# mLSTM and MLP boundaries of a two-block transformer kernel: result banks claimed later, scaled copies ahead of the next weight half, the first weight unit taken tile by tile over two columns

## What is computed

```python
for l in range(DEPTH):
    ada = cond @ ada_w[l] + ada_b[l]
    sh1, sc1, g1, sh2, sc2, g2 = jnp.split(ada, 6, axis=-1)
    h = modulate(rmsnorm(x, norm_g[l, 0]), sh1, sc1)       # x * (1 + scale) + shift
    if l < N_A:
        y = mlstm_mixer(h, ...)      # q, k, v, gates = h @ w_in; recurrence; (hh * sigmoid(og)) @ w_out
    else:
        y = mla_mixer(h, ...)
    x = x + g1[:, None, :] * rmsnorm(y, norm_g[l, 1])
    h = modulate(rmsnorm(x, norm_g[l, 2]), sh2, sc2)
    y = jnp.square(jax.nn.relu(h @ mlp_w1[l])) @ mlp_w2[l]  # 1024 -> 4096 -> 1024
    x = x + g2[:, None, :] * rmsnorm(y, norm_g[l, 3])
```

## Time and profile before

| | us |
|---|---|
| median of 3 runs | 1192.52 |
| lowest, highest | 1192.41, 1194.96 |
| the profiled execution, span from its first to its last instruction | 1188.7 |
| PE busy (matmuls) | 1099.4 |
| DVE busy | 741.1 |
| ACT busy | 500.7 |
| PE, mean granted clock | 0.977 of full |

### The profile page before, as it was taken

The page is one execution under the profiler, slowest core; times in us unless marked ns, Lnnn a source line. Parts: engine busy times, 40 slices in busy tenths (PEclk is TensorE's granted clock), DMA queues, the critical chain, the costliest instruction groups (busy, mean ns, idle before and its releaser), DMA issues.

```text
span 1188.7 us, 19624 instructions
## 1 busy us (share of the span) xinstructions
PE 1099.4 (92%) x8492; PEld 899.8 (76%) x8492; DVE 741.1 (62%) x1145; ACT 500.7 (42%) x774; POOL 33.3 (3%) x30
## 2 busy tenths in 40 slices
PE   3999978899899997999999899999899898999997
PEld 2885468897668776877767699899757676998995
DVE  4662676864758958575567758767446566555544
ACT  3311312123354466445354545535243644554442
POOL 0000003310000010000000000000000000000000
PEclk9999989999999999899999999999999989999999
DMA  9373400520346550254433486776643534565520
GB/s 387 130 300 135 150 1 3 204 85 4 141 155 271 211 214 1 81 191 176 190 142 142 151 330 235 291 289 262 261 164 142 213 142 142 212 224 202 203 82 36
DMA packets 15078, 204.88 MB, mean 172 GB/s; under 512 B 1800, under 2 KB 1800, under 8 KB 2832
## 3 DMA queue, kind: packets, MB, share of 16 engines
q1 hardware_dynamic: 14256, 201.33, 44.9%
q10 hardware_dynamic: 736, 2.30, 0.5%
HBM read 202.57 MB, written 1.05 MB: 171 GB/s over the span
## 4 chain that ended last, share of the span: by engine, by line
PE 75%; DVE 15%; ACT 4%; DMA 3%; issue 2%; ACTq 0%; DVEq 0%
PE bank L432 15%; PE bank L434 15%; PE bank L433 15%; PE bank L391 6%; PE bank L677 5%; PE bank L479 5%; DMA ring<-in_stream 3%; DVE slot_parts L1721 2%; PE bank L536 2%; PE bank L506 1%; PE bank L492 1%; ACT arena L1266 1%; DVE arena L1835 1%; PE bank L659 1%; DVE small L1695 1%
## 5 line engine op out<-in xcount | busy, mean ns | idle before, releaser
L432 PE MATMUL bank<-page_parts 128*128 128x512 f32 (+1 forms) x1152 | 393.3, 341 | 10.9 <-DVE page_parts L1754 3.2
L1721 DVE TENSOR_TENSOR slot_parts<-ring,page_parts 128x2048 fp32r<-128x2048 f32 x104 | 237.0, 2289 | 124.3 <-ACT page_parts L1173 124.0
L1173 ACT ACTIVATE page_parts<-ring 128x2048 fp32r<-128x2048 f32 x104 | 197.5, 1909 | 142.2 <-PE bank L434 88.0
L432 PEld LDWEIGHTS bank<-page_parts 128*128 128x128 f32 x1152 | 221.3, 192 | 36.2 <-issue 9.1
L433 PE MATMUL bank<-slot_parts,page_parts 128*128 128x512 f32 x576 | 225.0, 391 | 0.0
L434 PE MATMUL bank<-page_parts 128*128 128x512 f32 x576 | 225.0, 391 | 0.0
L1232 ACT ACTIVATE arena<-bank 128x512 f32<-128x512 f32 (+1 forms) x142 | 78.9, 572 | 224.8 <-PE bank L479 66.6
L433 PE MATMUL bank<-page_parts 128*128 128x256 f32 x576 | 164.8, 286 | 0.0
L434 PE MATMUL bank<-page_parts,slot_parts 128*128 128x256 f32 x576 | 164.7, 286 | 0.0
L434 PEld LDWEIGHTS bank<-page_parts 128*128 128x128 f32 x576 | 108.5, 188 | 23.1
L433 PEld LDWEIGHTS bank<-slot_parts,page_parts 128*128 128x128 f32 x576 | 108.6, 189 | 21.3
(11 more groups left out here) (272 smaller groups left out, 1162.4 us busy)
## 6 DMA issues: line engine op xcount, KB each, us to landing
ring<-in_stream SPq DMA_DIRECT2D x95, 2048.0 KB, 8.2
arena<-in_x SPq DMA_DIRECT2D x2, 512.0 KB, 6.2
gn<-in_gn ACTq DMA_DIRECT2D x2, 512.0 KB, 8.5
out<-arena SPq DMA_DIRECT2D x2, 512.0 KB, 2.6
cc<-in_consts ACTq DMA_DIRECT2D x1, 898.0 KB, 6.2
pc<-in_params ACTq DMA_DIRECT2D x1, 287.5 KB, 7.2
gn<-in_head_sel ACTq DMA_DIRECT2D x1, 32.0 KB
pos_i<-in_positions ACTq DMA_DIRECT2D x1, 1.0 KB, 7.1
```

Of the source, the lines that this page charges most:

```text
L432: mm(out, a[0], b[0], start=start, stop=False)
L1173: act(unit_parts(n)[0], unit_values(n)[1], ACT.Copy).then_inc(ac.step("w_hi"), 1)
L1721: tt(unit_parts(n)[1], lo, hi, ALU.subtract).then_inc(dv.step("w_lo"), 1)
```

## The change

Five edits:

1. A new helper `both_halves` issues the first unit of a stage's first product: for each tile k it waits for the tile if needed, does the three products for the first column half and then for the second, and goes on to the next tile. It is used for the first unit of q2 and of `("up", l, 0)`, 48 matmuls each; the number of matmuls is the same. Only the very first matmul of the bank opens it (`start`).
2. In an MLP the claims of banks 0 to 3 are moved from ahead of the first matrix to the first `down`.
3. In an MLP ACT does its eight scaled copies first and the rounding copy of the unit two ahead after them; the copy of the turned columns (L1240) stays behind both.
4. At the mLSTM input the explicit rounding copy `split(ahead(("q2", 0)))` is taken out; the loop that follows the scaled copies does it anyway, now behind the turned columns.
5. On DVE the second unit of `wo_c` is cut right behind `h2T`, ahead of the modulation and the diagonal.

```diff
+            def both_halves(b, W, src, wait):
+
+                for k in range(KT):
+                    pe.wait_ge(sem(wait[0]), wait[1] + k // 2 + 1)
+                    for half in range(2):
+                        out, w, a = b[:, half * T:(half + 1) * T], [w[:, k, half * P:(half + 1) * P] for w in W], [a[:, k, :] for a in src]
+                        mm(out, w[0], a[0], start=k == half == 0, stop=False, skip_group_check=True)
+                        mm(out, w[0], a[1], start=False, stop=False, skip_group_check=True)
+                        ins = mm(out, w[1], a[0], start=False, stop=k == KT - 1, skip_group_check=True)
+                return ins
+
             def split_T(name, src, pages, wait=None, between=None):
...
-                    for half in range(2):
+                    if wait and i == 0:
+                        ins = both_halves(b, W, src, wait)
+                    for half in range(0 if not wait or i else 2, 2):
                         for k in range(KT):
-                            if wait and i == half == 0:
-                                pe.wait_ge(sem(wait[0]), wait[1] + k // 2 + 1)
...
                 rotation["banks"] = [4, 5, 6, 7]
-                for tb in range(TB):
-                    for half in range(2):
-                        claim(("mlp", l, tb, half), 2 * tb + half)
...
                 def down(n):
                     split_panel(("w2", l, n), (3, 4, 14))
+                    if n == 0:
+                        for tb in range(TB):
+                            for half in range(2):
+                                claim(("mlp", l, tb, half), 2 * tb + half)
...
             def mlp(l):
+                mod_scaled(f"hT_m{l}", (1, 4)[l], hT2)
                 split(unit_of["up", l, 0, 0] + AHEAD)
-                mod_scaled(f"hT_m{l}", (1, 4)[l], hT2)
                 ada_turned()
...
             x_squares("wo_b")
-            split(ahead(("q2", 0)))
             ada_direct()
...
             split_h("h2T", H2_PAGES)
+            split(unit_of["wo_c", 0] + 1)
             modulation(6, 12, (1,))
             gate_diagonal(1)
             split(unit_of["wo_c", 1] + 1)
```

## The result

The changed kernel runs in 1177.39 us (median of 4 runs, 1176.87 to 1179.65), beside 1193.74 for the kernel before on the same chip; the ratio is 0.9866, with a 95% interval of 0.9853 to 0.9879. The direction was right and the size was not: 1180.7 was forecast, with a range down to 1178.7. Over all executions measured in the study, before has a mean of 1192.5 (84 runs, 1186.2 to 1198.1), the changed kernel 1177.9 (10 runs, 1175.4 to 1180.9): 14.6 us, uncertain by 1.2, where 11.8 were forecast. One execution of edit 3 alone took 2211.36 us, with PE busy for 2169.9 us under a recorded granted clock of 1.00; it is left out of every figure here and was not explained. The profiled execution of the changed kernel has a span of 1175.1 beside 1188.7, 13.6 less.

What follows compares the result with a forecast made beforehand. The prediction took PE's own time to bound the kernel, with idle at the boundaries removable: 8.2 us of waits plus 3.6 of clock, 11.8 off 1192.5, gave 1180.7 us, with a range of 1178.7 to 1184.4.

Steps and rivals of the forecast that it cites:

- What bounds the kernel: Whole kernel: PE makes up 75% of the chain, DVE 15%; a boundary is worth what PE idles there.
- mLSTM input: Ahead of q2: scaled copies start at 511.0, q2 2.7 us earlier, and 1.2 of half clock goes.
- the tile-by-tile order: First units of q2 and both MLPs: costs nothing, keeps 1.05 us of tile stalls per boundary from coming back.
- Output product: mLSTM layer's output product: PE's wait of 1.36 us for a weight unit goes wholly, taken as 1.4.
- The MLPs: Both MLP inputs: PE starts 2.0 and 2.1 us earlier, and 1.2 of half clock goes at each.
- gives its start back: Rival, first MLP: PE waits at the third panel and loses at most 2.0 + 1.2; 1183.9 us, chance 0.10.
- Clock at the boundaries: mLSTM input and both MLP starts: half-clock stretches go, 1.2 us each, 3.6 in all.
- The rivals in which the half clock stays: At both MLPs, 1183.1 us, or at the mLSTM input too, 1184.3; chance together 0.22.
- Gaps and clock further on fall elsewhere: Rival, loop over the heads: the half-clock stretch behind 576 goes, 1.7 us more, 1179.0; chance 0.12.
- the base: Starting time of the sum: profiled span 1188.7 plus 3.8 us taken as unchanged, so gains come off 1192.5.

Runs made afterwards that it cites:

- claims_only: The kernel before with only the claims of banks 0 to 3 moved to the first `down` in each MLP: ratio 0.9959, 4.9 us faster.
- copies_first_look: The kernel before with only the MLPs' scaled copies put ahead of the rounding copy, executed again for its profile: idle 3.66 and 3.78; first execution's ratio 1.0024.
- before_filled: The kernel before with unread extra matmuls in its large gaps, including those at the mLSTM input and both MLP inputs: 1184.40 us, ratio 0.9943.
- the filled one: The changed kernel with unread extra matmuls in its remaining large gaps: 1172.75 us, ratio 0.9839 to the kernel before.

## Why the prediction was wrong

**What bounds the kernel: right.** Each place that it named as PE's idle gave its time, and nothing outside them became late. The other engines' busy times are the same within 0.1 us.

**mLSTM input: right.** Forecast 2.7 of wait and 1.2 of clock, 3.9; measured 2.56 at the start (516.01 to 513.45) and 1.34 in the 48 matmuls behind it (7.16 to 5.82), 3.90. That the sum fits to the digit is luck: the wait was 0.1 too high and the clock 0.1 too low. The scaled copies began at 511.09, forecast 511.0; the low part of the next unit is ready at 519.0, forecast 519.1. That the tile-by-tile order costs nothing and keeps about 1.0 a boundary from coming back (1.05 in the prediction, 0.98 measured) holds: nothing alone, 2.9 of stalls with the rest.

**Output product: right in its wait, 0.3 short.** The idle went wholly, and the stage gained 1.65 where the row shows 1.36. Two parts make the difference. The idle of a row is counted from the end of the matmul before it, which lasts 0.39, while the next one usually starts after 0.23: 0.16 more. And the first matmul behind the gap has its follower after 0.33 (636.43 to 636.76) where 0.23 is usual: 0.10 more. 1.36 + 0.16 + 0.10 = 1.62. I had counted the idle alone.

**The MLPs: right.** 3.36 and 3.40 where 3.2 and 3.3 stood. In the first the wait gave 1.87 for 2.0 and the clock 1.49 for 1.2, in the second 2.06 for 2.1 and 1.40 for 1.2. PE began the first 0.16 behind DVE's first cut; shifted by the 7.20 gained before it, that is 666.61, forecast 666.5. The claims were the wait, as claims_only shows, and edit 3 needs edit 2, as copies_first_look shows; edit 2 alone leaves 0.65 and 0.44 of idle. The rival "gives its start back" did not come true: from the mark of 681.75 to a matmul at 850.13 before takes 168.38, the changed kernel from 671.19 to 839.64 takes 168.45. The rest of the 0.36 of the table's fifth row lies behind the first MLP and is within what one profile differs from another: from the 97th matmul of the first MLP to the transposes of the second's input, two profiles of before take 310.6 and 312.1, four of the changed kernel 310.8 to 311.1.

**Clock at the boundaries: right in kind, small in size.** The prediction took 13 slow matmuls, 1.2 us, at each, from one trace. Over the profiles that have those gaps the counts are 12 to 27 at q2, some 16 to 24 at the first MLP, 13 to 16 at the second. Against the changed kernel's 5.82 the first 48 matmuls take on average 1.56, 1.65 and 1.47 us longer, 4.7 in all where 3.6 was forecast; in the first profile of before it is 4.2. The rivals in which the half clock stays are out: it is full at all three in all four profiles of the changed kernel. The Trainium skill, "TensorE: Matmul & The Clock Gate", Part 4, would have kept all three, since transposes don't count as PE being busy; the trace doesn't agree with what I drew from it: behind 1.97 us of transposes and 1.05 of turned columns the clock is 1.00 at 513 to 515.

**What failed is the clock term of the sum, above all the stretch in the loop over the heads, which was put at nothing.** "Gaps and clock further on fall elsewhere", with the stretch behind 576 worth 1.7, was given 0.12 and kept out of the forecast. It was worth 1.65 in the profile of the changed kernel, and with 9 in 10 against 1 in 4 it is worth some 1.1 on average. The three boundaries, written as 3.6, gave 4.2 in the first profile and 4.7 on average. I had read one trace of before as if its half-clock stretches were fixed parts of it. They are draws: behind the same 1.72 at 342 and the same 1.17 at 576 the half clock is there in one execution and not in the next, and the kernel's own runs reach from 1186.2 to 1198.1 for the same program. The range made the same mistake. Its lower end, 1178.7, lay only 0.3 below the case that gives up the heads' stretch, while 0.5 of clock at the boundaries was missing too and the median is itself uncertain by about one.

The account: 12.0 from the two traces without the heads, which holds 4.2 of clock, 0.5 more for the mean of 4.7, and 1.1 for the heads is 13.6 of the 14.6 measured. Most of the last 1.0 may be chance in a part where no edit stands: the transposes ahead of q2 begin at 509.9 on average in the four profiles of the changed kernel (508.76 to 511.03), and at 510.7 in nine profiles of kernels in which PE has the same instructions up to there (509.12 to 512.79), 0.8 later. It is seen in the clock from 300 to 340 us, which has a mean of 0.87 in six of eleven profiles without the full change and unfilled there, 0.96 in the others and in all four of the changed kernel. Whether four profiles without the longer stretch there are chance, I leave open.

**A smaller error** stands in the base. I took 3.8 us as lying outside the span. In every run of the study whose span is known it is about 1.8 (1.76 to 1.97). The other 2.0 was the profiled execution being faster than its kernel's mean. It didn't change the number, which was taken off the median, but it hid that this execution had fewer slow stretches than most, so that counts from it were low.

## What to carry to other kernels

On an engine that is nearly always busy, a gap costs its idle time, where it goes wholly some 0.26 us more for the overlap and the slow first matmul that are lost with it (seen once, in the output product), and a share of a half-clock stretch behind it; take that share over several profiles and not from one. Edits on one wait don't add: the copies' order loses 2.9 us while the claims stand and gains 0.8 by the trace once they are gone, and the tile-by-tile order is worth nothing until the start is early, then 3. Where a gap can't be closed, filling it with matmuls that nothing reads was worth 5 us here. It did not always hold: at the mLSTM input of before_filled, with 1.04 of idle left, the half clock came all the same.

## What I had not expected of the hardware

- The same program shows half clock at different places from run to run. In the output product of the RWKV layer, behind the same gap of 1.72, it was full in the first trace of before and half for 13 matmuls of 512 columns in two of four of the changed kernel, which made that stretch 2.2 us longer. The Trainium skill says in "TensorE: Matmul & The Clock Gate", Part 1, that the number of slow matmuls of one kernel varies from run to run; the 12 to 27 at q2 agree.
- Alternating between two column halves of one PSUM bank every three matmuls costs nothing: 0.12 us a matmul of 256 columns, as without it.
- The mean granted clock goes with the time: 0.9753 over the runs of before, 0.9812 of the changed kernel, 0.9873 of the filled one. The filled one's four runs lie within 1.2 us and before_filled's four within 1.8, where two sets of four of the unfilled changed kernel lie within 2.8 and 4.6.
